# Where the squares of a norm are summed: on VectorE first, or by TensorE alone

## The reference

```python
def rms_norm(x, gain):
    y = xf * lax.rsqrt(jnp.mean(xf * xf, axis=-1, keepdims=True) + EPS)
    return (y * gain).astype(x.dtype)
def pre_norm(z, gain, mod, k):
    return rms_norm(z, gain) * (1 + mod[:, 3 * k + 1]) + mod[:, 3 * k]
h = h + 0.5 * mod_l[:, 2] * swiglu(pre_norm(h, norm_g[i, 0], mod_l, 0), ffn_w_in[i, 0], ffn_w_out[i, 0])
```

## Time and profile before

| | |
|---|---|
| median of 3 runs | 3136.11 us |
| profiled execution: its own time | 3135.86 us |
| profiled execution: span | 3134.2 us |
| TensorE matmul busy | 3019.6 us (96%) |
| VectorE busy | 1811.6 us (58%) |
| ScalarE busy | 859.2 us (27%) |

### The profile page before, as it was taken

How to read it: one execution, slowest core, us unless ns; L and a number is a source line. 1 busy time by engine, 2 the same in 40 slices (tenths; PEclk the granted TensorE clock), 3 DMA queues, 4 the chain that set the end, 5 groups by cost and what they waited for, 6 DMA issues and landing times.

```text
span 3134.2 us, 42265 instructions
## 1 busy us (share of the span) xinstructions
PE 3019.6 (96%) x17512; PEld 2624.0 (84%) x17512; DVE 1811.6 (58%) x2632; ACT 859.2 (27%) x1184; POOL 36.7 (1%) x73
## 2 busy tenths in 40 slices
PE   6999999999989899999999999999899999999999
PEld 4888888877877788888888888888788888888887
DVE  4675655765665676565674456566654646564454
ACT  3211111353454422111132112113322323242221
POOL 0000000000000000000000000000000000000000
PEclk8999999999999999999999999999899999999999
DMA  6332332111011143232321222232111212123222
GB/s 245 135 127 94 114 107 107 54 48 54 28 54 41 41 175 121 94 120 94 113 82 60 79 109 107 94 111 76 54 56 52 81 40 81 49 73 107 94 92 82
DMA packets 40984, 277.81 MB, mean 89 GB/s; under 512 B 4352, under 2 KB 5632, under 8 KB 8000
## 3 DMA queue, kind: packets, MB, share of 16 engines
q1 hardware_dynamic: 31024, 205.85, 18.2%
q0 software_dynamic: 9872, 70.72, 6.2%
HBM read 274.45 MB, written 2.10 MB: 88 GB/s over the span
## 4 chain that ended last, share of the span: by engine, by line
PE 88%; DVE 7%; ACT 2%; issue 2%; DMA 0%; SPq 0%; DVEq 0%; ACTq 0%
PE ps L311 28%; PE ps L313 28%; PE ps L312 28%; PE ps L630 2%; PE ps L339 1%; DVE wl L1303 1%; DVE act_buf L1387 1%; ACT wh L913 1%; DVE xnl L1391 1%; DVE irms L1594 0%; PE ps L325 0%; DVE ssum L1366 0%; DMA ada_w<-ada 0%; PE ps L357 0%; ACT xnh L944 0%
## 5 line engine op out<-in xcount | busy, mean ns | idle before, releaser
L311 PE MATMUL ps<-xnh,wl 128*128 128x512 f32 (+1 forms) x3040 | 1062.0, 349 | 28.4 <-DVE wl L1303 15.6
L312 PE MATMUL ps<-xnl,wh 128*128 128x512 f32 (+1 forms) x3040 | 1052.3, 346 | 0.0
L313 PE MATMUL ps<-xnh,wh 128*128 128x512 f32 (+1 forms) x3040 | 1050.8, 346 | 0.0
L311 PEld LDWEIGHTS ps<-xnh,wl 128*128 128x128 f32 x3040 | 580.2, 191 | 111.1 <-DVE wl L1303 17.4
L313 PEld LDWEIGHTS ps<-xnh,wh 128*128 128x128 f32 x3040 | 580.6, 191 | 70.3
L312 PEld LDWEIGHTS ps<-xnl,wh 128*128 128x128 f32 x3040 | 580.9, 191 | 67.9 <-issue 1.0
L1303 DVE TENSOR_TENSOR wl<-raw,wh 128x2048 fp32r<-128x2048 f32 (+2 forms) x183 | 402.3, 2199 | 142.0 <-ACT wh L913 141.7
L913 ACT ACTIVATE wh<-raw 128x2048 fp32r<-128x2048 f32 (+2 forms) x178 | 326.7, 1835 | 564.8 <-PE ps L313 564.8
L1445 DVE SCALAR_TENSOR_TENSOR h<-ps,coef,h 128x512 f32<-128x512 f32 x624 | 371.7, 644 | 105.4 <-PE ps L313 103.9
L311 PE MATMUL ps<-hidh,wl 128*128 128x512 f32 (+1 forms) x1232 | 422.2, 343 | 3.3 <-DVE h L1403 3.3
L313 PE MATMUL ps<-hidh,wh 128*128 128x512 f32 (+1 forms) x1232 | 423.2, 344 | 0.0
(11 more groups left out here) (240 smaller groups left out, 2987.9 us busy)
## 6 DMA issues: line engine op xcount, KB each, us to landing
raw<-weights SPq DMA_DIRECT2D x183, 1024.0 KB, 4.8
adaw<-ada POOLq DMA_DIRECT2D x64, 1024.0 KB, 5.1
ada_w<-ada SPq DMA_DIRECT2D x8, 1024.0 KB, 20.2
h<-x_in SPq DMA_DIRECT2D x1, 2048.0 KB, 8.8
c_act<-c_rows POOLq DMA_DIRECT2D x2, 1024.0 KB, 5.1
out<-h SPq DMA_DIRECT2D x8, 256.0 KB, 2.0
h<-x_in SPq DMA_DIRECT2D x1, 1024.0 KB, 27.8
cs<-rope_mla POOLq DMA_DIRECT2D x1, 512.0 KB, 3.4
```

The lines of the kernel that those rows point to most:

```text
L311: mm(dst, lhs[1][rows], rhs[0][rows], start=first, stop=False)
L312: mm(dst, lhs[0][rows], rhs[1][rows], start=False, stop=False)
L313: return mm(dst, lhs[0][rows], rhs[0][rows], start=False, stop=last)
```

## The change

In the ends that TensorE's `last_y` makes, for the first part, every squared block is summed by TensorE with a group of its own (`square_sum`), accumulated over the eight blocks in PSUM. The group for block m-2 stands behind y(m), the last two behind y(0) and y(1) of the second part, where `norm_sums` stood. ScalarE (`square_alone`) squares block m into half m % 2 of `act_buf` and waits, from m = 2 on, until TensorE has summed the square that lay there. VectorE adds no squares for this part. The second part, the start of the kernel and the end of the attention are as they were.

```diff
+        sq_summed = sem("sq_summed")
...
+            def square_sum(m, part):
+
+                t0, n = part
+                pe.wait_ge(sq_done, c.next(sq_done))
+                ins = quarter_sums(7, L, act_buf[:, m % 2, t0:t0 + n], n, m == 0, m == KD - 1)
+                ins.then_inc(sq_summed if m < KD - 1 else ms_full, 1)
...
                     y(m, parts[0], A_BANKS[m % 3], 0).then_inc(y_full, 1)
+                    if m >= 2:
+                        square_sum(m - 2, parts[0])
                 for m in range(KD):
...
                     y(m, parts[1], B_BANKS[m // 2], L * (m % 2)).then_inc(y_full, 1)
-                    if m == 1:
-                        norm_sums(0, parts)
+                    if m < 2:
+                        square_sum(KD - 2 + m, parts[0])
                     if m == 4:
                         norm_spread(0, parts)
...
+            def square_alone(m, part):
+
+                t0, n = part
+                act.wait_ge(y_added, c.next(y_added))
+                if m >= 2:
+                    act.wait_ge(sq_summed, c.next(sq_summed))
+                fn(act_buf[:, m % 2, t0:t0 + n], h[:, m, t0:t0 + n], ACT.Square).then_inc(sq_done, 1)
...
                 for m in range(KD):
-                    square(m, parts[0])
-                norm_root(0, parts)
+                    (square_alone if early is None else square)(m, parts[0])
+                if early is None:
+                    c.next(sq_summed)
+                norm_root(0, parts, early is None)
...
                     add_part(m, parts[0], A_BANKS[m % 3] if early is None else O_BANKS[m % 4])
-                    if m >= 2:
+                    if m >= 2 and early is not None:
                         add_square(m - 1, parts[0])
+                if early is None:
+                    c.next(sq_done, KD)
```

More of the change, by code:

```diff
@@ L930, in sqrt_table, with norm_root @@
                 fn(table[:], eps[:], ACT.Sqrt)
-            def norm_root(i, parts=STREAMS):
+            def norm_root(i, parts=STREAMS, alone=False):
                 n = parts[i][1] // 4
-                c.next(sq_added)
+                if not alone:
+                    c.next(sq_added)
                 act.wait_ge(ms_full, c.next(ms_full))
```

## The result

| | before | changed |
|---|---|---|
| median | 3135.81 us (5 runs, 3135.0 to 3136.31) | 3152.11 us (5 runs, 3151.72 to 3153.11) |
| ratio, 95% interval | | 1.0053, 1.0039 to 1.0068 |
| span of the profiled execution | 3134.2 us | 3150.1 us |
| VectorE busy | 1811.6 us | 1798.2 us |
| TensorE matmul records | 17512 | 17704 |

The change costs 16.3 us by the medians and 15.9 between the two profiled executions. 14.4 were forecast, and 3152.1 lies in the range of 3142 to 3157.

What follows compares the result with a forecast made beforehand. TensorE was taken as the bound at the stage ends: 3.8 us more at each of three ends (11.3) plus 3.0 at the 256-token end make 14.4, so 3150.5 us; range 3142 to 3157.

Steps and rivals of the forecast that it cites:

- The bound: At the stage ends, TensorE is full and the norm chain starts from its sums; work ahead of them moves everything behind.
- the two later waits: TensorE's waits of 0.35 and 0.85 us in the next stage's norm, forecast to give nothing back.
- The removed adds: Six VectorE adds per end, 4.1 us beside TensorE's products; removing them was forecast to gain nothing, square(7) being late next.
- The 0.28: TensorE's wait in us, at the first end's sums, that the last VectorE add was said to end.
- the pair's 0.93: Cost in us of the two joined norm-sum groups at an end before the change, their wait included.
- sum(0): First group, between y(2) and y(3): 0.66 us waiting for square(0) plus 0.33 to y(3), together 1.0 per end.
- One interruption: One group of sums between large products at 512 tokens: 0.53 us, bounds 0.24 and 0.67; sum(1) to sum(6) together 3.2.
- No waits at sum(1) to sum(7): At each end, TensorE reaches these groups after their squares have ended, so they add no waiting.
- The end of 256 tokens: The fourth end, behind the retention: 3.0 us more, between 0.8 and 4.0, with 0.42 per interruption.
- The clock: Rival, chance 0.13: longer TensorE waits drop the clock at three ends, 1.7 us each, 5.1 more, 3155.6 us in all.
- Nearly free: Rival, chance 0.11: a group costs only its streaming, 0.24 us (0.13 at 256 tokens); 5.8 in all, 3141.9 us.
- VectorE is the bound: Rival, chance 0.06: TensorE has room at the ends, so the sums fill waits; some 3135.2 us, not slower.

Runs made afterwards that it cites:

- e3_lag3: The changed kernel with block m-3's group behind y(m), a third buffer of squares and the last two groups joined: 3149.23 us, first end 15.45.
- e5_before_4banks: The kernel before with a fourth PSUM bank for y of the first part, so y(3) need not wait for `add_part`(0): 3134.22 us, first end 11.95.
- e1_joined: The changed kernel with all eight groups of sums in one place, behind y(1) of the second part: 3141.56 us, first end 13.59.

## Why the prediction was right

- **The bound.** TensorE is full from y(3) to the norm's first results, and all that follows starts from the sums. Right: the two later waits kept their length (0.35, 0.84), and what was put ahead of the sums is in the length of the ends.
- **The removed adds, counted as nothing.** Right, shown by leaving them out of one kernel (L 12.25 against 12.19) and putting them back into the other (16.25 against 16.28), and so was the reason given, square(7) late next. The 0.28 that the prediction gives as the wait for them holds 0.13 that passes without any wait; in its sum the 0.28 stands inside the pair's 0.93, so nothing hangs on that.
- **sum(0), 1.0 us.** Measured 1.01 (y(3) 1.82 instead of 0.81 behind `add_part`(0)). e3_lag3 took that wait away and got back what the working says, to 0.05.
- **One interruption, 0.53 at 512 tokens.** Mis-sized by little: 0.57. It had been built from a pair, 0.77, less a group of 0.24; but the pair is one interruption of 0.57 and a further group at 0.20, and the row of eight gives 0.22 for a further group. Six of them, and the last one, are 0.3 more per end than forecast, and 4.09 instead of 3.78 comes out. The 0.57 stands between the 0.53 and the bound of 0.67. That it has a fixed part of about 0.3 was right, and is shown to be the change of width.
- **No waits at sum(1) to sum(7).** Right: y(4) to y(7) come evenly, every 1.94.
- **The end of 256 tokens, 3.0.** Measured 3.28; y(m) came every 1.15 at full clock, 0.46 of it the interruption, where 0.42 was forecast.
- **The clock.** A rival with a chance of 0.13 and 5.1 us came true in part: at one of the three ends, for 1.5 us, and there in all four kernels with the long wait. The 14.4 have no such stretch in them, and one of the prediction's own signs of being wrong, a clock that falls at an end where it was 1.00, did appear.
- **The closeness of the total is in part luck.** The four ends without the clock are 15.5, 1.1 more than the 14.4 forecast; the clock adds 1.5; the places between the ends take 1.1 off again, and no run shows that this comes from the change.
- **The other rivals** fell. "Nearly free" has 0.24 for an interruption: that is what a single product without a change of width costs, and four narrow ones cost 0.57. "VectorE is the bound" is false in this layout and becomes true in e5_before_4banks, where TensorE comes 1.35 us earlier (the second part's y(0) stands 6.44 behind `add_part`(0), at 597.14, instead of 7.79): there the adds delay `add_part`(7).

## What to carry to other kernels

Before work is moved from an engine with slack to one without, ask who waits for it: here VectorE's 4.1 us of adds per end were waited for 0.15 us, and the next event was 0.06 behind. A few narrow matmuls in a stream of wide ones cost more than twice what they stream, so join them into one row. To make them full width would save the change of width but not the time here, since one such product covers a quarter of the tokens. Put a reduction of a block's result behind the next products that are ready, not in front of them.

## What the runs showed of the hardware

- Going from products of 128 columns of the array to 32 and back costs 0.32 us beyond the streaming: one narrow float32 product of 128 tokens 0.56, four of them in different columns 0.57, one of full width 0.24. In a joined row a further group of four costs 0.22 (1.88 for eight in e1_joined, 0.35 for one).
- At the third end a wait of TensorE of 1.82 us, 1.16 before, was followed by a stretch of low clock and 1.5 us of loss in all four kernels that have it (3.4 us at 0.51 in the changed one); waits of 1.74 and 1.75 at their first two ends were not. What apart from the wait's length sets the third end apart these runs don't show.
